# A hybrid attention, RWKV-7 and HGRN2 layer with experts on one core: order of the 64x64 matmuls between row halves

## The chip, the core and the metric

The kernel runs on one core of a Trainium2 chip. TensorE does the matmuls, reading its weights and moving data from SBUF and writing PSUM banks of 128 partitions by 512 f32; VectorE (DVE) and ScalarE (ACT) copy and process what lies in the banks, GpSimd (POOL) issues small transfers, and SyncE (SP) issues the large ones. The metric is the device time of one execution in microseconds; the median of the runs counts.

TensorE takes a matmul on a part of its array: the partitions that the operands lie in are its row part, the output partitions its column part. A "tile" here is such a part. With operands of 64 partitions and 64 output partitions there are four of them: row half 0 or 1 with column half 0 or 1. "Own" means that both halves have the same number, "other" that they differ.

## What is computed

Two groups of 128 tokens, a prompt and a sample, go through one layer with the same weights. Heads are split among attention, RWKV-7 and HGRN2; then come an output projection and 32 experts of which each token uses 4.

```python
# RWKV-7, both directions d
S = S * w_t + (S @ a_t) b_t^T + v_t k_t^T ;  y_t = S @ r_t
# HGRN2, chunkwise, both directions
att = einsum('ntd,nsd,ntsd->nts', q, k, dec) ;  o = att @ v + (q * exp(b)) @ S_before
# layer
x = x + gate1 * (concat(att, rwkv, hgrn) @ w_out)
x = x + gate2 * moe(norm(x))          # top 4 of 32, 1024 wide, clamped SwiGLU
```

The prompt starts from zero states, the sample from given ones. All is f32.

## The kernel before

The program is written by hand for each engine, in the order in which the engine runs it; semaphores join the engines. The eight PSUM banks are rotated: `open_bank` waits until the job that had the bank six jobs ago was read, `filled` signals a job as complete, `after` waits until it was read. Loops over s (0 the prompt, 1 the sample) and over two directions d are unrolled, and the four heads n lie in pairs, head n in row half n % 2 where its transposed data are used.

The sequence of TensorE is: modulation and input projections (to about 160 us), the mixers of the prompt, mixed with the input projections and the first levels, then the mixers of the sample (to about 338 us), the output projection (L938), the router, and from about 403 us a loop over the 32 experts (L1135, L1155), whose six weight blocks of 2 MB each stream through a ring of six slots. A slot is asked for again (L379) when its matmuls are done. The ring's memory serves as working memory of the mixers before, so that the second half of `w_out` is loaded into slot 0 only when `hg_done` is given, behind VectorE's copy L1708 of the last HGRN2 sum.

For each group the delta rule is solved with a 128-token triangle split into two halves of 64 rows: five levels of merges build an inverse (`rw_level_w` L667 and `rw_level_xy` L682, which alternate between the row halves), and then come the functions of this case, in this order for both groups:

- `rw_right`: right hand sides, matmuls with AKd (own, L717) and AKo (other, L721) and, for the sample, the initial state (L711). ScalarE then copies two blocks (L1267).
- `rw_first`: the first half solved (L734), in direction 0 row half 0, in direction 1 row half 1.
- `hg_scores(s, 2)`: HGRN2 scores of one pair of heads in one direction: one matmul for the pair of halves (`hg_off`, L832) and eight for four levels (L839), for each of two row halves q.
- `rw_carry` (L745), `rw_early_y` (L757 state, L763 own, L766 other), `rw_second` (L777), `hg_scores(s, 3)`, `rw_out` (L788 own, L790 other).
- for the prompt `rw_pairs` of the sample (L623, L634, L644) follows, and `hg_sum` (L856 state, L862 own, L865 other) later; for the sample `hg_sum` follows at once.

[...] There are 16 fences in all. The state matmuls have 128 output partitions (64x128); two for each direction and row half.

## Time and profile before

| | us |
|---|---|
| median of 3 runs (1364.95 to 1370.54) | 1368.74 |
| the profiled execution | 1370.94 |
| its span, first to last instruction | 1368.7 |
| TensorE matmuls busy | 1231.2 (90%) |
| VectorE busy | 311.4 (23%) |
| ScalarE busy | 228.7 (17%) |

[...] The DMA moves 427 to 429 GB/s from about 445 us to the end. [...]

### The profile page before, as it was taken

The page shows a single profiled execution, that of the slowest core. Times are in us where ns is not written, and L with a number is a line of the kernel's source. Part 1 is how long each engine was busy: PE and PEld are TensorE (multiplying, and loading weights), DVE is VectorE, ACT ScalarE, POOL GpSimd, SP SyncE. Part 2 cuts the span into 40 slices and gives each one's busy share as a digit, 9 for nine tenths or more (in the row PEclk, how much of TensorE's full clock was granted, in tenths as well). Part 3 has the DMA queues.
Part 4 walks back from the last instruction along what each step waited for, and adds up shares of the span by engine and source line. Part 5 has one row for each costly group of instructions (what it writes and reads, how often), then busy time and mean ns, then how long its engine had stood idle before and what let it go on. Part 6 is the DMA issues. An engine that isn't in the chain of part 4 may idle for free.

```text
span 1368.7 us, 17187 instructions
## 1 busy us (share of the span) xinstructions
PE 1231.2 (90%) x7074; PEld 513.1 (37%) x7074; DVE 311.4 (23%) x629; ACT 228.7 (17%) x381; POOL 37.9 (3%) x69
## 2 busy tenths in 40 slices
PE   3988999788869999999999999999999999999994
PEld 1333578668343333333233333233333333333331
DVE  1200655652230112111121111112111112111113
ACT  2110344343121111111111111111111111111112
POOL 0300000000000000000000000000000000000000
PEclk9998997885858999999999999999999999999998
DMA  9966300003945999999999999999999999999991
GB/s 372 321 253 219 140 1 3 10 4 124 386 169 245 428 427 428 426 429 429 428 426 427 428 429 426 428 427 428 429 427 427 428 427 428 428 427 427 428 429 76
DMA packets 44241, 459.93 MB, mean 336 GB/s; under 512 B 5113, under 2 KB 7329, under 8 KB 16433
## 3 DMA queue, kind: packets, MB, share of 16 engines
q1 hardware_dynamic: 41152, 451.98, 78.9%
q0 software_dynamic: 2576, 6.35, 1.7%
q10 hardware_dynamic: 480, 1.13, 0.2%
q8 instruction: 25, 0.41, 0.1%
q14 instruction: 8, 0.06, 0.0%
HBM read 457.96 MB, written 1.47 MB: 336 GB/s over the span
## 4 chain that ended last, share of the span: by engine, by line
DMA 50%; PE 42%; DVE 4%; ACT 2%; issue 1%; DVEq 0%; SPq 0%; ACTq 0%
DMA ring<-in_moe_w_gu_dram 45%; PE bank L1135 15%; DMA ring<-in_w_mod_dram 5%; PE bank L567 4%; PE bank L1155 4%; PE bank L938 2%; PE bank L544 2%; PE bank L682 1%; PE bank L1098 1%; PE bank L1113 1%; PE bank L557 1%; PE bank L839 1%; PE bank L1125 1%; PE bank L824 1%; PE bank L667 1%
## 5 line engine op out<-in xcount | busy, mean ns | idle before, releaser
L1135 PE MATMUL bank<-ring,proj 128*64 128x512 f32 x2048 | 459.0, 598 | 33.7 <-DMA ring<-in_moe_w_gu_dram 33.7
L1135 PEld LDWEIGHTS bank<-ring,proj 128*64 128x64 f32 x2048 | 140.3, 137 | 350.9 <-issue 274.7
L1155 PE MATMUL bank<-ring,proj 128*64 128x512 f32 x1024 | 233.8, 598 | 11.9 <-DVE proj L2011 11.9
L2002 DVE TENSOR_SCALAR proj<-bank 128x512 f32<-128x512 f32 x32 | 22.1, 692 | 484.6 <-PE bank L1135 484.6
L1491 ACT ACTIVATE proj<-proj 128x512 f32<-128x512 f32 x32 | 20.2, 630 | 605.3 <-DVE proj L2002 605.3
L1155 PEld LDWEIGHTS bank<-ring,proj 128*64 128x64 f32 x1024 | 69.0, 136 | 131.8 <-issue 131.8
L567 PE MATMUL bank<-ring,hT 128*128 128x512 f32 (+2 forms) x224 | 92.6, 571 | 4.3 <-DVE hT L1813 2.7
L2014 DVE COPY proj<-bank 128x512 f32<-128x512 f32 x32 | 22.1, 691 | 249.1 <-PE bank L1155 249.1
L1098 PE MATMUL bank<-h_nat,proj 128*64 128x512 f32 x264 | 64.0, 607 | 0.0
L1113 PE MATMUL bank<-proj 64*128 64x512 f32 x256 | 63.6, 615 | 0.0
L567 PEld LDWEIGHTS bank<-ring,hT 128*128 128x128 f32 x224 | 43.9, 200 | 52.3 <-issue 41.8
L544 PE MATMUL bank<-ring 128*32 128x512 f32 x192 | 30.9, 775 | 17.0 <-DMA ring<-in_w_mod_dram 16.7
L1106 PEld LDWEIGHTS bank<-const_sb,proj 128*128 128x128 f32 x260 | 34.3, 212 | 25.8 <-DVE proj L2009 24.3
L510 POOL DMA_DIRECT2D param_sb<-in_moe_b_gu_dram x32 | 17.7, 553 | 893.6 <-PE bank L1125 893.6
L1491 ACT ACT_TABLE_LOAD x32 | 41.1, 1283 | 0.6
L1106 PE MATMUL bank<-const_sb,proj 128*128 128x128 f32 x260 | 40.8, 300 | 0.0
L1113 PEld LDWEIGHTS bank<-proj 64*128 64x128 f32 x256 | 22.0, 186 | 41.0 <-issue 41.0
L938 PE MATMUL bank<-ring,hT 128*128 128x512 f32 x64 | 30.3, 635 | 6.9 <-DMA ring<-in_w_out_dram 6.1
L1125 PE MATMUL bank<-param_sb,const_sb 1*64 1x512 f32 x256 | 35.7, 627 | 0.8 <-ACT proj L1487 0.8
L1487 ACT ACTIVATE proj<-bank 128x512 f32<-128x512 f32 x33 | 19.7, 597 | 86.9 <-PE bank L1106 86.9
L2011 DVE COPY proj<-bank 128x512 f32<-128x512 f32 x32 | 22.1, 692 | 50.1 <-PE bank L1106 50.1
L1098 PEld LDWEIGHTS bank<-h_nat,proj 128*64 128x64 f32 x264 | 19.1, 139 | 38.2 <-issue 37.8
(333 smaller groups left out, 890.7 us busy)
## 6 DMA issues: line engine op xcount, KB each, us to landing
ring<-in_moe_w_gu_dram SPq DMA_DIRECT2D x128, 2048.0 KB, 24.4
ring<-in_moe_w_down_dram SPq DMA_DIRECT2D x64, 2048.0 KB, 21.7
ring<-in_w_mod_dram SPq DMA_DIRECT2D x12, 2048.0 KB, 10.1
ring<-in_w_in_dram SPq DMA_DIRECT2D x5, 2048.0 KB, 17.0
ring<-in_w_out_dram SPq DMA_DIRECT2D x2, 2048.0 KB, 7.7
const_sb<-in_constants_dram POOLq DMA_DIRECT2D x1, 2450.0 KB, 14.4
ring<-in_w_in_dram SPq DMA_DIRECT2D x1, 1536.0 KB, 6.6
ring<-in_w_in_dram SPq DMA_DIRECT2D x1, 1024.0 KB, 5.4
```

What stands on the lines that cost most here:

```text
L544: mm = pe.matmul(b[32 * q:32 * q + 32, :], keep["c_silu"].rearrange("p (c m) -> p c m", m=32)[:, k], ring[:, slot, kc * 2048 + q * 512:kc ...
L567: mm = pe.matmul(b[:, 0:w], hT[:, s, c, :], wv[:, c, :], start=(c == 0), stop=(c == KC - 1))
L938: mm = pe.matmul(b[:, :], hT[:, s, c, :], wv[:, c % 4, 512 * part:512 * part + 512], start=(c == 0), stop=(c == KC - 1))
L1098: mm = pe.matmul(b_misc[CAP * half:CAP * half + CAP, :], moe["hot"][:, CAP * s:CAP * s + CAP], h[:, s, 512 * half:512 * half + 512], start ...
L1106: mm = pe.transpose(out[:, P * c:P * c + P], cols[:, c, :], ident)
L1113: mm = pe.matmul(acc[2 * s + half][:, :], moe["scat"][rows, P * s:P * s + P], moe["y"][rows, :], start=False, stop=False, skip_group_check ...
L1125: mm = pe.matmul(b[CAP * half:CAP * half + CAP, :], ones[32 * q:32 * q + 1, 0:CAP], param[32 * q:32 * q + 1, 3 * D:3 * D + 512], start=Tru ...
L1135: mm = pe.matmul(b[CAP * half:CAP * half + CAP, :], xT[:, k % 4, k // 4, :], ring[:, j, 2048 * kc + o + 512 * half:2048 * kc + o + 512 * h ...
L1155: mm = pe.matmul(b_down[CAP * half:CAP * half + CAP, :], aT[:, k % 4, k // 4, :], ring[:, 4 + j, D * kc + 512 * half:D * kc + 512 * half + ...
L1491: A(moe["sig"], moe["glu"], ACT.Sigmoid, scale=ALPHA).then_inc(sem("sig_sb"), 1)
L2002: ts(moe["glu"], bank[4][:, :], LIMIT, None, ALU.min).then_inc(sem("glu_sb"), 1)
L2011: dve.tensor_copy(moe["actT"], bank[6][:, :]).then_inc(sem("actT_sb"), 1)
```

## The change

In `rw_right`, `rw_early_y`, `rw_out`, `hg_scores` and `hg_sum` the passes are no longer one for each row half. In one pass come the matmuls whose output half is their own row half, in the other those whose output half is the other one; inside a pass the row halves alternate. A fence stands between the passes. The state matmuls are split in two of 64 output partitions, the own one in the first pass and the other one in the second (`state_part`, and `begin` in `hg_sum`). `rw_out` does the pass with the other half first. In `rw_first`, `rw_carry` and `rw_second` the loops over heads and directions are exchanged, which makes their row halves alternate too.

```diff
+            def state_part(s, b, y, col, own, begun):
+
+                for n2 in range(2):
+                    for d in range(2):
+                        for r in range(2):
+                            o = r if own else 1 - r
+                            n = 2 * n2 + r
+                            mm = pe.matmul(b[part64(o), col(d, n)], T[part64(r), d, 0, n2, y, part64(o)], s0[part64(r), 2 * d + n2, :],
+                                           start=o not in begun, stop=False, skip_group_check=True)
+                            begun.add(o)
+                return mm
...
             def rw_right(s):
...
-                for r in range(2):
-                    if s:
-                        for d in range(2):
-                            for n in (r, 2 + r):
-                                cols = slice(256 * d + DH * n, 256 * d + DH * n + DH)
-                                pe.matmul(b[:, cols], T[part64(r), d, 0, n // 2, 0, :], s0[part64(r), 2 * d + n // 2, :],
-                                          start=not begun, stop=False, skip_group_check=True)
-                                begun |= {0, 1}
-                    for d in range(2):
-                        for n in range(4):
-                            cols = slice(256 * d + DH * n, 256 * d + DH * n + DH)
-                            mm = pe.matmul(b[part64(r), cols], AKd[part64(r), d, n, 0, :], vcols(s, n)[part64(r)],
+                    state_part(s, b, 0, col, True, begun)
+                for d in range(2):
+                    for n in range(4):
+                        for r in range(2):
+                            mm = pe.matmul(b[part64(r), col(d, n)], AKd[part64(r), d, n, 0, :], vcols(s, n)[part64(r)],
                                            start=r not in begun, stop=False, skip_group_check=True)
                             begun.add(r)
-                            if d == r:
-                                mm = pe.matmul(b[part64(1 - r), cols], AKo[part64(r), n, 0, :], vcols(s, n)[part64(r)],
-                                               start=1 - r not in begun, stop=False, skip_group_check=True)
-                                begun.add(1 - r)
-                    if r == 0:
-                        fence(mm)
+                fence(mm)
+                if s:
+                    state_part(s, b, 0, col, False, begun)
+                for n in range(4):
+                    for r in range(2):
+                        mm = pe.matmul(b[part64(1 - r), col(r, n)], AKo[part64(r), n, 0, :], vcols(s, n)[part64(r)],
+                                       start=False, stop=False, skip_group_check=True)
                 mm.then_inc(sem("rw_R1"), 1)
...
             def rw_first(s):
...
-                for d in range(2):
-                    for n in range(4):
+                for n in range(4):
+                    for d in range(2):
...
             def rw_out(s):
...
-                for r in (1, 0):
-                    for n in range(4):
-                        cols = slice(DH * n, DH * n + DH)
-                        for d in range(2):
-                            mm = pe.matmul(b[part64(r), cols], LRd[part64(r), d, n, 1, :], Ru[part64(r), d, n, :],
-                                           start=False, stop=False, skip_group_check=True)
-                        mm = pe.matmul(b[part64(1 - r), cols], LRo[part64(r), n, 1, :], Ru[part64(r), r, n, :],
-                                       start=False, stop=(r == 0), skip_group_check=True)
-                    if r == 1:
-                        fence(mm)
+                for n in range(4):
+                    for r in range(2):
+                        mm = pe.matmul(b[part64(1 - r), DH * n:DH * n + DH], LRo[part64(r), n, 1, :], Ru[part64(r), r, n, :],
+                                       start=False, stop=False, skip_group_check=True)
+                fence(mm)
+                for n in range(4):
+                    for d in range(2):
+                        for r in range(2):
+                            mm = pe.matmul(b[part64(r), DH * n:DH * n + DH], LRd[part64(r), d, n, 1, :], Ru[part64(r), d, n, :],
+                                           start=False, stop=(d == 1), skip_group_check=True)
                 filled(mm, "rw_y", s)
...
             def hg_scores(s, u):
...
-                for q in range(2):
-                    Uq = U[part64(q), u % 2]
-                    mm = pe.matmul(over[part64(d), DH * q:DH * q + DH], Uq[:, 1, 0, part64(d)], Uq[:, 0, 0, part64(1 - d)],
-                                   start=True, stop=True)
-                    if q:
-                        filled(mm, "hg_off", s, u)
+                def inside(own):
                     for l in range(1, 5):
-                        for blk in range(2):
-                            o = P * (l - 1) + DH * q
-                            mm = pe.matmul(b[part64(blk), o:o + DH], Uq[:, 1, l, part64(blk)], Uq[:, 0, l, part64(blk)],
-                                           start=True, stop=True)
-                    if q == 0:
-                        fence(mm)
-                filled(mm, "hg_att", s, u)
+                        for q in range(2):
+                            Uq, o, blk = U[part64(q), u % 2], P * (l - 1) + DH * q, part64(q if own else 1 - q)
+                            mm = pe.matmul(b[blk, o:o + DH], Uq[:, 1, l, blk], Uq[:, 0, l, blk], start=True, stop=True)
+                    return mm
+
+                off(0)
+                fence(inside(True))
+                filled(off(1), "hg_off", s, u)
+                filled(inside(False), "hg_att", s, u)
```

`rw_early_y` and `hg_sum` are changed as `rw_right` is. Nothing is changed on the other engines.

Below is TensorE's order in `rw_right` and the start of `rw_first` of the sample. Line numbers are those of the kernel that each belongs to; `x_res` holds the transposed factors T, `ring` AKd, AKo and the state, `proj` the values. Before (L711 state, L717 own, L721 other; a shape reads output partitions by columns):

```order
L711 MATMUL bank<-ring,x_res 128x64 x3
L717 MATMUL bank<-proj,ring 64x64
L721 MATMUL bank<-proj,ring 64x64
...
L717 MATMUL bank<-proj,ring 64x64 x4
L711 MATMUL bank<-ring,x_res 128x64 [waits pe_fence]
L711 MATMUL bank<-ring,x_res 128x64 x3
L717 MATMUL bank<-proj,ring 64x64 x5
L721 MATMUL bank<-proj,ring 64x64
...
L734 MATMUL bank<-hT,ring 64x64 [waits bank_free2,rw_Ysb,rw_Rsb]
```

After (L704 state, L726 own, L734 other, L744 `rw_first`):

```order
L704 MATMUL bank<-ring,x_res 64x64 x7
L726 MATMUL bank<-proj,ring 64x64 x16
L704 MATMUL bank<-ring,x_res 64x64 [waits pe_fence]
L704 MATMUL bank<-ring,x_res 64x64 x7
L734 MATMUL bank<-proj,ring 64x64 x8
L744 MATMUL bank<-hT,ring 64x64 [waits bank_free2,rw_Ysb,rw_Rsb]
```

Two state matmuls of 64 output partitions stand for one of 128, and the matmuls with AKo have moved behind the fence.

The second place is the end of `rw_out` and the `hg_sum` of the sample, on TensorE. Before (L788 and L790 `rw_out`, L856 state, L862 own, L865 other):

```order
L788 MATMUL bank<-hT,h_nat 64x64 x2
L790 MATMUL bank<-hT,h_nat 64x64
L856 MATMUL bank<-ring 128x64 [waits bank_free3,bank_free0,bank_free2,bank_free4,hg_attD]
L856 MATMUL bank<-ring 128x64 x3
L862 MATMUL bank<-proj,ring 64x64 x2
L865 MATMUL bank<-proj,ring 64x64
...
L856 MATMUL bank<-ring 128x64 [waits pe_fence]
L856 MATMUL bank<-ring 128x64 x3
```

After (L803 own pass of `rw_out`, L872 state, L882 own, L891 other):

```order
L803 MATMUL bank<-hT,h_nat 64x64 [waits pe_fence]
L803 MATMUL bank<-hT,h_nat 64x64 x15
L872 MATMUL bank<-ring 64x64 [waits bank_free3,bank_free0,bank_free2,bank_free4,hg_attD]
L872 MATMUL bank<-ring 64x64 x7
L882 MATMUL bank<-proj,ring 64x64 x16
L872 MATMUL bank<-ring 64x64 [waits pe_fence]
L872 MATMUL bank<-ring 64x64 x7
L891 MATMUL bank<-proj,ring 64x64 x8
```

The waits are the same, in front of the same functions; own and other matmuls stand apart, on either side of the fence.

## Rows read from the trace of the kernel before

**Rows 1.** Chain that ended last: shares by engine; pieces (start us, length us, what).

```profile
DMA 50%; PE 42%; DVE 4%; ACT 2%; issue 1%; DVEq 0%; SPq 0%; ACTq 0%
...
337.58 7.68 DMA ring<-in_w_out_dram
...
627.80 25.30 DMA ring<-in_moe_w_gu_dram
```

**Rows 2.** Waits of the load queue, 280 to 460 us: total, times, longest (us).

```profile
SPq L379 <- PE bank L1135: 62.5, 7, 44.0
```

**Rows 3.** Timeline: start us, us, engine, line, operation, count [idle before <- releaser].

```profile
220.66 0.27 PE L717 MATMUL bank<-proj,ring 64*64 64x64 f32 x1
...
223.89 1.17 PE L734 MATMUL bank<-hT,ring 64*64 64x64 f32 x13 [0.89 <-ACT hT L1267]
...
234.89 1.28 ACT L1203 ACT_TABLE_LOAD   x1
...
251.91 0.27 PE L862 MATMUL bank<-proj,ring 64*64 64x64 f32 x1
...
303.37 1.10 PE L711 MATMUL bank<-ring,x_res 64*128 64x64 f32 x8
...
314.62 1.96 PE L757 MATMUL bank<-ring,x_res 64*128 64x64 f32 x8
...
329.68 1.96 PE L856 MATMUL bank<-ring 64*128 64x64 f32 x8
...
337.52 0.42 DVE L1708 COPY mix<-bank 128x256 f32<-128x256 f32 x1 [5.40 <-PE bank L865]
```

**Rows 4.** Chain that ended last, within the mixers of both groups.

```profile
223.06 0.38 ACT hT L1267
...
239.22 0.44 DVE small L1645
...
246.15 1.10 PE bank L644 x32
...
254.27 1.88 PE bank L682 x62
```

**Rows 5.** Stretches: us, busy (records) of PE, others, granted clock, DMA.

```profile
223.10:223.90 0.80, 0.01 (x1) 0.01 (x1) 0.80 (x2) 0.71 (x2) 0.00 (x0) 1.00 0.00 0
223.90:225.00 1.10, 1.10 (x19) 1.10 (x22) 1.10 (x4) 0.00 (x0) 0.00 (x0) 0.57 0.00 0
...
303.40:305.60 2.20, 2.14 (x34) 1.94 (x33) 2.08 (x4) 0.00 (x0) 0.00 (x0) 1.00 0.00 0
305.60:309.00 3.40, 3.40 (x32) 3.23 (x32) 0.69 (x1) 0.00 (x0) 0.00 (x0) 0.56 0.38 89
...
285.00:289.00 4.00, 2.04 (x65) 1.00 0.01 2
```

**Rows 6.** Timeline of TensorE: runs that alternate, and L824, at either clock.

```profile
213.29 0.63 PE L839 MATMUL bank<-ring 64*64 64x64 f32 x15
...
276.36 3.68 PE L682 MATMUL bank<-ring 64*64 64x64 f32 x64 [3.73 <-DVE ring L1633]
279.96 2.59 PE L824 MATMUL bank<-const_sb,proj 128*128 128x512 f32 x4
...
283.56 1.56 PE L824 MATMUL bank<-const_sb,proj 128*128 128x512 f32 x4
...
287.08 2.08 PE L682 MATMUL bank<-ring 64*64 64x64 f32 x64 [1.96 <-DVE ring L1633]
```

**Rows 7.** Runs on one tile: chain piece at the high clock, timeline at the low.

```profile
221.34 0.47 PE bank L717 x8
...
228.94 0.53 PE L763 MATMUL bank<-proj,ring 64*64 64x64 f32 x3
...
229.36 0.86 PE L763 MATMUL bank<-proj,ring 64*64 64x64 f32 x3
```

**Rows 8.** Half a microsecond of TensorE with clock, DMA share and GB/s.

```profile
316.00:316.50 0.50, 0.50 (x3) 0.50 0.13 49
```

More of the change, by code:

```diff
@@ L851, in hg_sum, with begin @@
                 begun = set()
-                for r in range(2):
-                    if s:
-                        for n in (r, 2 + r):
-                            for d in range(2):
-                                pe.matmul(b[:, DH * n:DH * n + DH], inter[part64(r), 2 * d + n // 2, :], hst[part64(r), 2 * d + n // 2, :],
-                                          start=not begun, stop=False, skip_group_check=True)
-                                begun |= {0, 1}
-                    for n in range(4):
-                        cols = slice(DH * n, DH * n + DH)
-                        for d in range(2):
+                def begin(own):
+                    for n2 in range(2):
+                        for d in range(2):
+                            for r in range(2):
+                                o, n = r if own else 1 - r, 2 * n2 + r
+                                pe.matmul(b[part64(o), DH * n:DH * n + DH], inter[part64(r), 2 * d + n2, part64(o)],
+                                          hst[part64(r), 2 * d + n2, :], start=o not in begun, stop=False, skip_group_check=True)
+                                begun.add(o)
+                if s:
+                    begin(True)
+                for n in range(4):
+                    cols = slice(DH * n, DH * n + DH)
+                    for d in range(2):
+                        for r in range(2):
                             mm = pe.matmul(b[part64(r), cols], attD[part64(r), d, n, :], v[part64(r), cols],
@@ L864, in hg_sum @@
                             begun.add(r)
+                fence(mm)
+                if s:
+                    begin(False)
+                for n in range(4):
+                    cols = slice(DH * n, DH * n + DH)
+                    for r in range(2):
                         mm = pe.matmul(b[part64(1 - r), cols], attO[part64(r), n, :], v[part64(r), cols],
-                                       start=1 - r not in begun, stop=(r == 1), skip_group_check=True)
-                        begun.add(1 - r)
-                    if r == 0:
-                        fence(mm)
+                                       start=False, stop=True, skip_group_check=True)
                 filled(mm, "hg_o", s)
```

46 lines of the change are left out of this document (25 added, 21 removed).

## The prediction

> **What bounds the kernel now.** I read the chain that ended last first. From about 628 us on it is a relay of weight transfers, 25.30 us for the first, with short matmuls between, the expert loop at the DMA's rate; the line of shares has DMA at half of the chain [rows 1]. That stream can't start before the loop frees its first ring slot: the load queue's longest wait, 44.0 us, is for L1135 [rows 2]. So the kernel is a mixer of about 338 us, an output part and a stream of fixed length in a row, and what the mixer ends earlier the whole ends earlier. At the mixer's end TensorE's last sums (L865) release one VectorE copy, at 337.52, and the second half of the output weights is requested only then: 7.68 us in which nothing else can start [rows 1, 3]. That transfer's length stays and its start moves.
>
> Inside the mixer two stretches of the changed lines lie on the chain. A, the prompt group: from L717 at 220.66 to the VectorE reduce L1645 at 239.22, which waited for TensorE; behind it a chain of VectorE work leads to L644 at 246.15 [rows 3, 4]. B, the sample group: L711 at 303.37 to that copy at 337.52, TensorE busy nearly throughout [rows 3]. [...]
>
> **Prices.** An f32 matmul leaves two records. [...] Matmuls with the initial state (L711, L757, L856) are 64x128: 8 records take 1.10 us at the high level and 1.96 at the low, 0.14 and 0.245 each [rows 3].
>
> [...]
>
> **The change, part by part.** Fences stay 16 in number, one to a block, and cancel. No DMA, VectorE, ScalarE or GpSimd instruction changes. What changes is the order, and each state matmul splits in two: 24 of 64x128 become 48 of 64x64, 96 records. No row shows such a 64x64 state matmul; it lies between 0.0296/0.054 (any alternating 64x64) and 0.14/0.245 (its own old price). I take the low end, since L717, also a small one with a 64-row weight and 64 columns, runs at it where it alternates. Pass two alternates row half 0 to columns 1 with row half 1 to columns 0 in one bank, also unseen in this order: between 0.0296 and 0.059, and I take the low end, by L682, which writes one bank from both row halves.
>
> A, rw_right: 48 records, now from 220.66 until ScalarE's copy at 223.06 [rows 3, 4], 2.40 us; then 48 x 0.0296 + 0.25 + 0.2 = 1.87. Saves 0.5. Two ScalarE copies follow, and the idle time of 0.89 before L734 stays [rows 3]. From 223.89 to 239.22, 15.33 us, run 16 + 36 + 16 + 48 + 16 + 36 + 48 = 216 records and 4 fences. Short one-tile runs (L734, L745, L777) were already mixed with their neighbours by the engine, so I price the whole. At the low clock: 216 x 0.054 + 4 x 0.33 + 0.3 = 13.3, saves 2.1. At the high clock: 216 x 0.0296 + 4 x 0.25 + 0.2 = 7.6, saves 7.7, of which 0.3 is lost, since ScalarE's two table loads of 1.28, begun behind the last hg_scores, then end later than VectorE's reduce and its followers [rows 3].
>
> hg_sum of the prompt group, at the high clock: 251.91 to 254.27 for 48 records [rows 3, 4]; then 48 x 0.0296 + 0.25 = 1.7, saves 0.6.
>
> B, 34.15 us now. rw_right has 80 records, 80 x 0.0296 + 0.45 = 2.8; ScalarE's copies 0.9; then 248 records and 4 fences; then hg_sum, 80 and a fence. High clock: 2.8 + 0.9 + (7.3 + 1.0) + 2.8 = 14.8, saves 19.3. With the clock low from rw_right's end: 3.0 + 0.9 + (13.4 + 1.3) + 4.9 = 23.5, saves 10.7.
>
> Behind B is the transfer. Its cover is the first half of the weights and two spreads, landed by 316 us, when the DMA share falls to 0.13 [rows 8]; with all of A and B gone they would land some 2 us before the new request, so they do not bind yet.
>
> **The clock decides the size.** With the clock as now: 0.5 + 2.1 + 0.6 + 10.7 = 13.9. With it high through A and B: 0.5 + 7.4 + 0.6 + 19.3 = 27.8. What the rows say: in A the clock fell at about 224, after a rw_right of which 16 records of 48 ran alone on a tile and 0.8 us of idle time. In 285 to 289 TensorE also idled for 1.96 us and then ran alternating records (L682) without a break, and the clock stayed at 1.00 [rows 5, 6]. In B it fell after L711, eight records in a microsecond. The changed blocks alternate as L682 does there, and even with the ScalarE gap they are denser than either stretch in which it fell. So I take the high level through both. Against it: dense alternating records alone did not raise a clock that was down (L682 at 276.36, 3.68 us, all slow), so one fall costs the rest of its stretch. There is also a giving back: with A short, TensorE finishes its L634 work early and waits some 4 us for VectorE before L644; an idle time of 3.73 us before L682 at 276.36 put that run and the next at the low clock, (3.68 - 2.08) + (2.59 - 1.56) = 2.6 us [rows 6]. I book 2.6 as lost: 27.8 - 2.6 = 25.2.
>
> The profiled execution took 1370.94, its span 1368.7; the median shown is 1368.74, 2.2 lower. By the execution 1345.7; against the median, which I forecast: 1368.74 - 25.2 = 1343.5.
>
> **Rivals.** 1. The clock stays down in B only: 0.5 + 7.4 + 0.6 - 2.6 + 10.7 = 16.6, 1352; in A only: 22.5, 1346. Chance 0.22 together. 2. The clock goes as now: 1354.8, or 1356.7 if it falls before B's rw_right (80 x 0.054 + 0.6 = 4.9 instead of 3.0). Chance 0.16. 3. Pass two does not run in parallel: 336 records at double price, 128 of them where the clock is high now (3.8 us) and 208 where it is low (11.2), 15.0 against 13.9: 1369.8, no change. For it: no row has this order within one bank; against it L745, whose two tiles are these and whose records came closer than one-tile pace. Chance 0.05. [...] 4. Slower: a state record keeps its old price, being bound by its fetch and not by its width. Then 32 x 0.14 + 64 x 0.245 = 20.1 us stand for 10.6 now and 4.4 in my sum: 13.9 - 15.7 = -1.8, 1370.5; all 96 at 0.245, 13.9 - 19.1 = -5.2, 1373.9. It decides from 0.19 us a record on. Chance 0.04. 5. The gain is absorbed behind the mixer, because the stream or the ring waits for something fixed: 1362 to 1369. Against it the 44.0 us wait and the transfer at 337.58. Chance 0.03.
>
> **Numbers.** The forecast has 0.5. The range for 8 in 10 reaches from 1338.5 (no giving back, and cheaper fences) to 1357 (rival 2 with its early fall). A measurement of this kernel tells 0.5%, 6.8 us, from no change. Faster by more: 0.5 + 0.22 + 0.16 and a little of rival 5, 0.89. Within 0.5%: rivals 3 and 5, most of 4, 0.09. Slower by more: 0.02, for rivals 3 and 4 at once.
>
> **What would show it.** The clock in the new trace: 1.00 from L717's successor to the end of B's sums confirms the forecast; 0.5 behind the first ScalarE gap gives rival 2. Blocks of 80 records should take 2.8 us (high) or 4.9 (low), rw_out 1.9 or 3.2. Pass-two rows at 0.059 show rival 3, state rows at 0.14 rival 4. The VectorE reduce L1645 should start near 231, B last 15 us instead of 34, the weight transfer still 7.7, and the expert loop unchanged behind it. Wrong would be: a TensorE wait for hg_attD before hg_sum, since VectorE's four masked copies (1.3 us) have only 1.7 us of rw_out to hide in; or a different pattern of low clock between 246 and 303, which can give or take some 3 us.

## The result, and the profile after

| | before | changed |
|---|---|---|
| median, us | 1368.69 (4 runs) | 1345.62 (4 runs, 1345.12 to 1348.24) |
| ratio, 95% interval | | 0.9826 (0.9803 to 0.985) |
| the profiled execution, us | 1370.94 | 1348.24 |
| its span, us | 1368.7 | 1346.1 |

The change takes 23.1 us off the median. From here on six lengths are read from the trace of every kernel: the start of A (first matmul of the prompt's `rw_right`), A (to VectorE's reduce), the time between A and B, B (first matmul of the sample's `rw_right` to VectorE's copy of the last HGRN2 sum), the transfer behind it, and the rest.

| | start of A | A | between | B | transfer | rest |
|---|---|---|---|---|---|---|
| before | 220.7 | 18.56 | 64.15 | 34.15 | 7.68 | 1023.4 |
| changed | 222.2 | 10.22 | 64.91 | 18.23 | 7.76 | 1022.7 |
| difference | +1.6 | -8.34 | +0.76 | -15.92 | +0.08 | -0.7 |

The sum is -22.6 us, the difference of the spans. The program ahead of A and behind the transfer is the same in both. The lengths come from one profiled execution of each kernel; their spans differ by 22.6 us, the medians by 23.1.

The page of the changed kernel: span; busy time of TensorE; granted clock in 40 slices, in tenths; the line of chain shares.

```profile
span 1346.1 us, 17283 instructions
...
PE 1207.8 (90%) x7122; PEld 489.6 (36%) x7122; DVE 311.7 (23%) x629; ACT 228.8 (17%) x381; POOL 37.9 (3%) x69
...
PEclk8988899798859999999999999999999999999997
...
DMA 51%; PE 41%; DVE 4%; ACT 2%; issue 1%; DVEq 0%; SPq 0%; ACTq 0%
```

The 96 more instructions are the 48 additional records of TensorE, each with its weight load. The 24 additional matmuls leave 48 records, two each; so do the 16 of L726, x16 in the order and x32 in the timeline below. Its chain that ended last, start and length in us, which answers to [rows 1]; and the longest wait of the load queue, which answers to [rows 2]:

```profile
315.64 7.76 DMA ring<-in_w_out_dram
...
605.84 24.85 DMA ring<-in_moe_w_gu_dram
```

```profile
SPq L379 <- PE bank L1158: 69.2, 9, 44.0
```

The frame of the prediction stands. The transfer has its old length and starts 21.9 us sooner, the expert stream its old length and starts 22.0 us sooner, and the wait behind it is 44.0 us as before.

Stretch A in the timeline of the changed kernel (start us, us, engine, line, what, count, in brackets the idle time before and who ended it; L726 and L734 `rw_right`, L744 `rw_first`, L797 and L803 `rw_out`, L644 `rw_pairs`; VectorE's L1668 is the reduce that was L1645, its L1721 copies the HGRN2 scores). It answers to [rows 3, 4, 7]:

```profile
222.22 1.15 PE L726 MATMUL bank<-proj,ring 64*64 64x64 f32 x32
223.43 0.68 PE L734 MATMUL bank<-proj,ring 64*64 64x64 f32 x16
224.99 0.51 PE L744 MATMUL bank<-hT,ring 64*64 64x64 f32 x10 [0.88 <-ACT hT L1290]
...
230.23 0.63 PE L797 MATMUL bank<-hT,h_nat 64*64 64x64 f32 x16
230.93 1.08 PE L803 MATMUL bank<-hT,h_nat 64*64 64x64 f32 x29
...
230.97 1.31 DVE L1721 COPY_PREDICATED ring<-const_sb,bank 128x128 f32<-128x128 int32 x4 [0.51 <-DVE ring L1721]
232.44 0.42 DVE L1668 TENSOR_REDUCE small<-bank 128x4 f32<-128x256 f32 x1 [0.15 <-DVE ring L1721]
...
239.38 1.85 PE L644 MATMUL bank<-x_res 64*64 64x128 f32 x32 [3.67 <-DVE ring L1643]
```

Sixteen records in 0.63 to 0.68 us, 32 in 1.10 to 1.15: at a granted clock of 1.00 that is about 0.03 a record, in the own passes (L726, L803) and the other ones (L734, L797) alike. At a fence (the last matmul of a pass signals, and TensorE waits for the signal) it takes longer: L734 starts 1.21 us behind L726's first record, 0.26 more than 32 x 0.0296. The reduce is no longer released by TensorE but by VectorE's own queue of four masked copies, 0.15 us behind the last of them. And L644 starts after 3.67 us of idle time and takes 1.85 us instead of 1.10.

Stretch B (L704 state, L772 and L780 `rw_early_y`, L788 `rw_second`, L872 state of `hg_sum`, L891 its other pass, L1731 the copy that was L1708):

```profile
297.35 0.68 PE L704 MATMUL bank<-ring,x_res 64*64 64x64 f32 x16
297.86 1.10 PE L726 MATMUL bank<-proj,ring 64*64 64x64 f32 x32
299.03 0.68 PE L704 MATMUL bank<-ring,x_res 64*64 64x64 f32 x16
...
303.56 1.10 PE L772 MATMUL bank<-proj,ring 64*64 64x64 f32 x32
304.73 0.68 PE L704 MATMUL bank<-ring,x_res 64*64 64x64 f32 x16
305.24 0.28 PE L780 MATMUL bank<-proj,ring 64*64 64x64 f32 x4
307.72 0.51 PE L780 MATMUL bank<-proj,ring 64*64 64x64 f32 x7 [2.20 <-issue]
...
315.58 0.42 DVE L1731 COPY mix<-bank 128x256 f32<-128x256 f32 x1 [0.30 <-PE bank L891]
```

A state record costs 0.03 us like any other (16 in 0.68 us, as for L734). Inside a run of matmuls that wait for nobody stands a gap of 2.20 us, put down to "issue": nothing that the profile shows ended it. This is the new thing in this trace.

The clock, by stretches (length; busy time and records of PE, PEld, DVE, ACT, POOL; granted clock; DMA share; GB/s):

```profile
222.20:232.40 10.20, 8.98 (x297) 8.13 (x296) 8.83 (x21) 6.43 (x16) 1.16 (x2) 1.00 0.02 4
232.40:239.40 7.00, 2.15 (x77) 1.82 (x70) 6.20 (x16) 1.02 (x2) 0.00 (x0) 1.00 0.01 2
239.40:242.90 3.50, 3.50 (x40) 2.84 (x42) 3.27 (x5) 1.41 (x5) 0.00 (x0) 0.53 0.00 0
...
297.40:305.50 8.10, 7.01 (x217) 6.40 (x217) 3.96 (x9) 2.54 (x7) 0.00 (x0) 1.00 0.46 156
305.50:307.70 2.20, 0.02 (x2) 0.00 (x0) 0.00 (x0) 0.00 (x0) 0.00 (x0) 1.00 0.99 402
307.70:311.00 3.30, 3.21 (x67) 3.02 (x67) 0.00 (x0) 1.25 (x4) 0.00 (x0) 0.52 0.78 310
```

All of A is at a granted clock of 1.00, against 0.51 in 223.9 to 239.2 before. B is at 1.00 until the end of the gap and at 0.52 in the 3.3 us behind it; the first half of the output weights comes in meanwhile (DMA share 0.99 in the gap). High and low, up and down stand here for 1.00 and 0.50: half microseconds of before, 305.0 to 306.5, show 1.00, 0.97 and 0.50, and a value between comes from a stretch in which the clock changes.

### The profile page after: what moved, and what is told of

The parts are those of the page before. It is cut to its first block, busy times and chain, and to the rows that moved or that the text cites. A ratio compares the mean times of both kernels' runs of the same rounds, so it can differ in the third digit from the quotient of the medians.

```text
span 1346.1 us, 17283 instructions
## 1 busy us (share of the span) xinstructions
PE 1207.8 (90%) x7122; PEld 489.6 (36%) x7122; DVE 311.7 (23%) x629; ACT 228.8 (17%) x381; POOL 37.9 (3%) x69
## 4 chain that ended last, share of the span: by engine, by line
DMA 51%; PE 41%; DVE 4%; ACT 2%; issue 1%; DVEq 0%; SPq 0%; ACTq 0%
DMA ring<-in_moe_w_gu_dram 46%; PE bank L1158 15%; DMA ring<-in_w_mod_dram 5%; PE bank L567 4%; PE bank L1178 4%; PE bank L961 2%; PE bank L544 2%; PE bank L682 1%; PE bank L1121 1%; PE bank L1136 1%; PE bank L557 1%; PE bank L1148 1%; PE bank L667 1%; DMA ring<-in_w_out_dram 1%; PE bank L1196 1%
## 5 line engine op out<-in xcount | busy, mean ns | idle before, releaser
L1178 PE MATMUL bank<-ring,proj 128*64 128x512 f32 x1024 | 233.9, 598 | 11.9 <-DVE proj L2034 11.9
```

Of the source, the lines that this page charges most:

```text
L1178: mm = pe.matmul(b_down[CAP * half:CAP * half + CAP, :], aT[:, k % 4, k // 4, :], ring[:, 4 + j, D * kc + 512 * half:D * kc + 512 * half + ...
```

## The experiments

The kernels in one table; a median of one run is marked (1). p1 to p4 shared one chip and its runs of before (median 1369.48), p5 to p8 another set (1369.72), p9 to p11 a third (1368.81), p12 a fourth (1369.48).

| | median | ratio (95%) | start of A | A | between | B | transfer | rest |
|---|---|---|---|---|---|---|---|---|
| p1_right | 1352.93 | 0.9866 (0.9834 to 0.9898) | 225.5 | 11.84 | 66.68 | 26.27 | 7.68 | 1018.1 |
| p2_split | 1359.84 | 0.9919 (0.9892 to 0.9947) | 221.2 | 18.32 | 67.67 | 25.20 | 7.47 | 1022.2 |
| p3_scores | 1365.75 | 0.9981 (0.9962 to 1.0) | 216.5 | 13.58 | 65.68 | 31.32 | 7.57 | 1022.1 |
| p4_prompt_only | 1358.05 | 0.9893 (0.9856 to 0.9931) | 221.2 | 10.22 | 64.93 | 33.60 | 7.64 | 1020.3 |
| p5_sample_only | 1357.07 | 0.9893 (0.9856 to 0.993) | 221.7 | 18.65 | 66.18 | 18.26 | 7.72 | 1023.0 |
| p6_wout_mid | 1344.3 | 0.9819 (0.978 to 0.9859) | 219.8 | 10.22 | 64.90 | 14.40 | 11.98 | 1022.0 |
| p7_wout_late | 1350.64 (1) | | 221.0 | 10.23 | 64.92 | 14.39 | 15.04 | 1022.8 |
| p8_clock_down | 1361.81 (1) | | 231.5 | 12.95 | 67.06 | 18.03 | 7.75 | 1022.3 |
| p9_wout_fence | 1345.52 | 0.9827 (0.9809 to 0.9845) | 220.9 | 10.20 | 64.92 | 14.90 | 9.63 | 1023.3 |
| p10_wout_scores | 1343.24 | 0.9812 (0.9789 to 0.9834) | 219.2 | 10.21 | 64.91 | 17.72 | 7.69 | 1022.8 |
| p11_old_right | 1349.63 | 0.9865 (0.9847 to 0.9883) | 221.5 | 11.78 | 63.50 | 18.43 | 7.69 | 1021.9 |
| p12_spread_first | 1342.77 | 0.9796 (0.9775 to 0.9816) | 220.7 | 10.22 | 64.91 | 14.39 | 7.95 | 1022.3 |

Two things are to be seen before any verdict. All lengths of a row come from one profiled execution. With all blocks changed A takes 10.20 to 10.23 us in every trace where the clock is up, to a few hundredths. But the start of A scatters from 216.5 to 225.5 (p8 delays it on purpose) and the rest from 1018.1 to 1023.4, in parts of the program that no kernel touches. So a total says no more than its interval, and the verdicts below go by the stretches.

### One part of the change alone: rw_right

```diff
@@ before, function rw_right only: replaced by the new one, with state_part
-                for r in range(2):
-                    if s:
...
+                if s:
+                    state_part(s, b, 0, col, True, begun)
```

> The kernel before with only rw_right in its new order. Pace alone (clock as in the kernel before): the prompt's rw_right 1.9 us instead of 2.4, the sample's 2.8 to 3.0 instead of 5.8, in sum 3.4 us faster, about 1365.3. Theory of the clock (what TensorE did in and right behind rw_right decides whether it falls): the granted clock stays at 1.00 behind 224 us too, and the unchanged functions then run at the high level; the prompt's stretch from there to VectorE's reduce takes 9 to 10 us instead of 15.3 and the whole gains 8 to 20 us, 1349 to 1361.

16.6 us by the medians (14 to 23 by the interval). The paces of the prediction give rw_right 0.5 us in A and 2.9 in B. The stretches shortened by 6.7 and 7.9. The windows of this kernel say why (same columns as above; A, then B in two parts):

```profile
225.50:237.40 11.90, 10.67 (x287) 9.80 (x287) 8.85 (x22) 6.80 (x16) 1.16 (x2) 1.00 0.01 3
304.10:314.00 9.90, 8.82 (x195) 8.07 (x195) 3.96 (x9) 2.54 (x7) 0.00 (x0) 1.00 0.56 204
...
315.00:330.30 15.30, 15.08 (x169) 14.04 (x167) 3.24 (x10) 5.29 (x8) 0.00 (x0) 0.50 0.13 50
```

So of the two expectations the one on the clock came. A block of 48 records, made denser, keeps the clock up through 11.9 us in which every other block is the old one (granted clock 1.00; 0.51 in before's 223.9 to 239.2). In A the clock is then worth 6.72 - 0.5 = 6.2 of the 8.3 us that the whole change gains; the order of all other blocks adds only 11.84 - 10.22 = 1.6. In B the clock holds for 10 us and falls in the old `rw_early_y`. The 2.20 us gap does not appear, although the transfer runs (DMA share 0.56).

The other kernels bear it out: in the five with the old `rw_right` in A and no added wait (before, p2, p3, p5, p11) the clock falls 3.2 to 3.7 us behind the start of A, and in none of the eight with the new one (changed, p1, p4, p6, p7, p9, p10, p12) does it fall in A.

### The split of the state matmuls alone

```diff
-                                pe.matmul(b[:, cols], T[part64(r), d, 0, n // 2, 0, :], s0[part64(r), 2 * d + n // 2, :],
-                                          start=not begun, stop=False, skip_group_check=True)
-                                begun |= {0, 1}
+                                for o in (r, 1 - r):
+                                    pe.matmul(b[part64(o), cols], T[part64(r), d, 0, n // 2, 0, part64(o)], s0[part64(r), 2 * d + n // 2, :],
+                                              start=o not in begun, stop=False, skip_group_check=True)
+                                    begun.add(o)
```

and the same in `rw_early_y` and `hg_sum`; a pass stays one row half.

> The kernel before with only the state matmuls of the sample split in two of 64 output partitions; the passes stay one for each row half, so that a pair alternates between column halves of the same row half. Theory that any two tiles run side by side: 96 records at 0.03 to 0.054 us, 3 to 5.2 us in place of 10.6, so 5.4 to 7.6 us faster, 1361 to 1363.5. [...] Rival, the price hangs on the record and not on its width: 3 to 13 us slower.

9.6 us by the medians, B shorter by 8.95, A as before. Its state runs at either clock (they stood at 1.10 and 1.96 for x8 in [rows 3]):

```profile
307.17 0.68 PE L712 MATMUL bank<-ring,x_res 64*64 64x64 f32 x16
...
316.70 1.12 PE L759 MATMUL bank<-ring,x_res 64*64 64x64 f32 x16
```

Sixteen narrow records in 0.68 where eight wide ones took 1.10, 1.12 where they took 1.96. There are six such blocks. The first took 1.10 and the second, with the clock falling in it, 1.65 us before; both take 0.68 now. The others went from 1.96 to 1.12: 0.42 + 0.97 + 4 x 0.84 = 4.75 us. The rest of the 8.95 is put down to the clock, for the other records: it fell 6.5 us behind the start of B, against 2.6 before. Both matmuls of a pair lie in one row half and still overlap: 16 records in 0.68 us, against 8 in 0.47 on one tile [rows 7].

### hg_scores alone

```diff
-                for q in range(2):
-                    Uq = U[part64(q), u % 2]
...
+                off(0)
+                fence(inside(True))
+                filled(off(1), "hg_off", s, u)
+                filled(inside(False), "hg_att", s, u)
```

> The kernel before with only hg_scores in its new order (8 calls). Theory: its pairs alternated already (between column halves), 0 within 0.7 us. Rival (only different row groups overlap): 7 us faster.

Ten runs, 1359.06 to 1371.25: 3.7 us less by the medians, the interval from 0 to 5.2, so a small gain is possible and the rival's 7 is excluded. One run of 15 records in this kernel:

```profile
213.82 0.63 PE L840 MATMUL bank<-ring 64*64 64x64 f32 x15
```

It is the 0.63 us of the kernel before [rows 6]: alternating row halves and columns together is no faster than alternating columns in one row half. The profiled execution is the fastest of the ten; in it the clock of A was down for 3.4 microseconds only, and A took 13.58 us. That the clock can come back inside A, in a kernel whose records have the old pace, was the first sign against a step of the prediction.

### One group alone

```diff
+            def rw_right(s):
+                (rw_right_new if s == 0 else rw_right_old)(s)
...
```

and so for all eight functions; p4 has the new ones for the prompt, p5 for the sample.

> All changed functions in their new order for the prompt group, in their old order for the sample group. Theory: the prompt's stretch shortens by 8.3 us as in the trace of the changed kernel, of which up to 2 us go again to a low clock after TensorE's longer wait before L644; 6 to 8.5 us faster, about 1361.5; the sample's stretch stays at 34 us. If the clock of the prompt's stretch had nothing to do with it: 2.6 + 0.6 = 3.2 us faster.

> All changed functions in their new order for the sample group, old for the prompt group. Theory: the prompt's stretch stays at 18.6 us with its low clock, the sample's shortens from 34.2 to 15 to 18.5 us because its clock stays high; 15.5 to 19 us faster, 1350 to 1353. If the pace alone did it (clock low behind its first block): 10.7 us faster, 1358.

A in p4 is the 10.22 us of the full change, and its B 33.60 us, at the low level from 300 us on. In p5 B is 18.26 us, again with a gap of 2.2 us at the same matmul, and A 18.65. So each group's stretch shortens by its own order alone, 8.3 and 15.9 us, and nothing is carried over. By medians p4 gained 11.4 and p5 12.7; of p5's 15.9, 2.0 were lost between A and B, where the clock was down for longer (mean granted clock 0.81, against 0.88 in 239.3 to 303.4 of before). Rows of p4's B and of p5 in the gap:

```profile
300.00:329.80 29.80, 28.56 (x320) 26.61 (x318) 4.43 (x14) 7.83 (x15) 0.00 (x0) 0.50 0.29 107
```

```profile
316.91 0.52 PE L864 MATMUL bank<-proj,ring 64*64 64x64 f32 x7 [2.23 <-issue]
```

### What the gap of 2.2 us is

In three kernels (the changed one, p5 and p8) it sits behind the second matmul of `rw_early_y`'s other pass, 8.2 us into B, while the transfer runs. The next two kernels are the changed one with the request of the first half of `w_out` put off, so that the transfer does not run there.

```diff
             sp.wait_ge(sem("cache_out"), 32)
+            sp.wait_ge(full[jobs["rw_u", 1] % ROT], jobs["rw_u", 1] // ROT + 1)
             ring_load(4, w_out[:, 0:4, :])
```

(p6, until `rw_second` is complete; p7 in the same way until `rw_out` is complete, job `rw_y`.)

> The changed kernel, but the load queue waits for the sample's rw_second before it asks for the first half of the output weights (and the spreads behind it). The profiled changed kernel has a gap of 2.20 us in the middle of rw_early_y of the sample in which TensorE waits for no other engine, while this transfer runs and one instruction fetch is among its packets. Theory that the fetch waits behind the transfer: the gap is gone, the sample's stretch is 15 to 16 us instead of 18.3, and the transfer of the second half ends 0 to 2 us later; in sum 0 to 3 us faster than the changed kernel. Rival, the gap has another cause: the stretch stays at 18.3.

> The changed kernel with the first half of the output weights asked for only after the sample's rw_out, when nearly all of the sample's stretch is over. Fetch theory: no gap in the stretch, 15 us from L704 to VectorE's copy; rival: a gap of about 2 us as before. The wait for the weights behind it grows from 7.7 to about 13 us, so the whole is 2 to 4 us slower than the changed kernel.

The same place in p6 (L781 and L789 are the L780 and L788 of above), and all of its B:

```profile
302.76 0.46 PE L781 MATMUL bank<-proj,ring 64*64 64x64 f32 x10
303.01 0.27 PE L789 MATMUL bank<-hT,ring 64*64 64x64 f32 x2
```

```profile
294.90:309.20 14.30, 13.00 (x410) 11.97 (x409) 7.23 (x19) 5.04 (x12) 0.00 (x0) 1.00 0.30 105
```

No gap, no fall of the clock, B 14.40 us. So the gap comes with the transfer at that time, and it costs 3.83 us: 2.20 itself, 1.6 by the clock behind it. But the second half of the weights now queues behind the first: 11.98 us in p6, 15.04 in p7. B with the transfer takes 26.4 and 29.5 us against 26.05: one wait has been traded for another.

### A place for the transfer

p9 and p10 look for the time at which the first half can run without that.

```diff
             sp.wait_ge(sem("cache_out"), 32)
+            sp.wait_ge(sem("pe_fence"), 13)
             ring_load(4, w_out[:, 0:4, :])
```

is p9 (the fence of the sample's `rw_early_y`); p10 waits instead for the bank of the sample's third `hg_scores`, job `("hg_att", 1, 2)`.

> The changed kernel; only the request for the first half of w_out is put off until the fence of the sample's rw_early_y, 7.4 us behind the start of stretch B (3.2 in the changed kernel, 8.9 in p6_wout_mid). My theory: the 2.20 us in which TensorE waits for nothing the profile shows is its next instructions arriving late behind this transfer's packets. The request now comes when that place is nearly reached and its packets flow over 1 us later, so no such gap, B 14.4 us. The two halves and the spreads then need 17.5 us from the first request, as in p6_wout_mid: 24.9 us from B's start to the landing of the second half against 26.05 in the changed kernel. Time 1344.5. Rival (the gap belongs to this place in the code whatever the DMA does): gap of 2.2 stays, B 18.2, landing 26.0, 1345.6.

> The same request put off only until the sample's third hg_scores is complete, 5.5 us behind the start of B. If the packets are not yet dense when TensorE's next instructions are fetched, no gap: B 14.4 us, landing at 5.5 + 17.5 = 23.0 us from B's start, 3.0 less than the changed kernel, 1342.6. If they are dense enough, the gap is back in part or whole and with it the low clock behind it: B up to 18.2 us, landing 26.0, 1345.6. The rival of p9_wout_fence expects 1345.6 here as well.

p9 came as my theory had it: no gap at the old place, B and transfer 24.6 us, 1.5 less than in the changed kernel. p10 went half each way. The old place has no gap, but a second one appears, in `hg_sum`, at a matmul where p9 has a trace of it (first row p10, second p9, of the same instruction):

```profile
308.16 0.24 PE L873 MATMUL bank<-ring 64*64 64x64 f32 x1 [1.63 <-issue]
```

```profile
308.46 0.21 PE L873 MATMUL bank<-ring 64*64 64x64 f32 x1 [0.26 <-issue]
```

Two fixed places in the program, then. The traces say more of them if TensorE's own records are counted one by one in order of start (weight loads, matmuls, semaphores and the like). Before the gap stand 5313 of them in the changed kernel, in p5 and in p8, before the second place 5569 in p9 and p10: 256 more. And p8 has one instruction more ahead of B, its wait for the copies. There the gap lies one instruction earlier in the program, with four weight loads of `rw_early_y`'s other pass in front of it and not five (first row changed kernel, second p8):

```profile
305.18 0.25 PEld L780 LDWEIGHTS bank<-proj,ring 64*64 64x64 f32 x5
```

```profile
319.37 0.20 PEld L780 LDWEIGHTS bank<-proj,ring 64*64 64x64 f32 x4
```

So the place hangs on the count of instructions and not on a matmul or its data. That fits instructions that are themselves fetched by DMA, piece by piece: the page has a DMA queue of kind "instruction" with 25 packets, of 16,384 bytes each. One of them runs in 299.0 to 299.5 us of p6, 4.6 us into B, where no load is under way, and in 305.0 to 305.5 us of the changed kernel, 8.0 us into B, amid the load (first row p6, second changed; packets, MB, share of 16 engines):

```profile
q8 instruction: 1, 0.02, 15.8%
```

```profile
q8 instruction: 1, 0.02, 11.6%
```

The packet records of nine kernels, in us behind the start of B, with the time at which TensorE comes to the place and the time at which it goes on:

| | place | packet starts | landed | TensorE comes | goes on |
|---|---|---|---|---|---|
| changed | first | 7.96 | 8.88 | 8.18 | 10.37 |
| p5 | first | 7.95 | 8.88 | 8.18 | 10.40 |
| p8 | first | 7.87 | 8.80 | 8.18 | 10.28 |
| p10 | second | 11.37 | 12.33 | 12.19 | 13.82 |
| p9 | second | 10.03 | 10.91 | 12.19 | 12.45 |
| p6 | first | 4.57 | 5.83 | 8.2 | no gap |
| p7 | first | 4.83 | 6.21 | 8.2 | no gap |
| p1 | first | 7.89 | 8.82 | 11.3 | no gap |
| p11 | first | 9.63 | 10.61 | 12.3 | no gap |

In all five gaps, from 0.26 to 2.23 us long, TensorE goes on 1.5 us behind the landing, and where there is no gap it comes to the place later than that. The packet itself is late when the load is in flow: TensorE passes the instruction 256 ahead of the first place at 4.0 us in the changed kernel, p5 to p10, and the packet starts 0.6 to 1.1 us later in p6, p7, p9 and p10 and 3.9 to 4.0 us later in the changed kernel, p5 and p8. So the theory of the instruction fetch agrees with these traces in place, time and size. No record names the packet's content; that it holds TensorE's instructions is inferred. p1 and p11 have the load and no gap because their TensorE, slower on its way there, comes later.

The last kernel takes the load queue apart instead: the two spreads of the gate (1 MB) need neither place nor data from the mixer.

```diff
+            sp.wait_ge(free[jobs["rw_T", 1, 1, 1] % ROT], jobs["rw_T", 1, 1, 1] // ROT + 1)
+            for s in range(2):
+                spread(gate1[:, s, :], 2 * D, s, "gate1_in")
             sp.wait_ge(sem("at_done"), 1)
             sp.wait_ge(sem("cache_out"), 32)
+            sp.wait_ge(sem("pe_fence"), 13)
             ring_load(4, w_out[:, 0:4, :])
-            sp.wait_ge(free[jobs["rw_T", 1, 1, 1] % ROT], jobs["rw_T", 1, 1, 1] // ROT + 1)
-            for s in range(2):
-                spread(gate1[:, s, :], 2 * D, s, "gate1_in")
```

> The changed kernel with the load queue in another order: the two spreads of the gate (1 MB) are requested as soon as their place is free, before the attention of the sample ends, and the first half of w_out (2 MB) at the fence of the sample's rw_early_y as in p9_wout_fence. My theory (TensorE's next instructions come late only behind dense packets, and the second half of w_out waits for what is queued ahead of it): B as in p9_wout_fence or shorter, 14.4 to 14.9 us, with no gap of 2.2 us, and the second half takes 7.7 us after its request instead of 9.63, since only 2 MB are ahead of it: 22.3 us from B's start to its landing, against 24.5 in p9_wout_fence and 26.05 in the changed kernel. 1345.6 - 3.7 = 1341.9. Rival 1: the early spreads meet another fetch of instructions and bring a gap of about 2 us there: 1344. Rival 2 (the transfer's packets are not what matters): nothing is saved, 1345.6.

Its load queue, the chain at the transfer, and B:

```profile
214.61 0.82 SPq L383 DMA_DIRECT2D param_sb<-mod_rows  x2
```

```profile
310.31 7.95 DMA ring<-in_w_out_dram
```

```profile
295.90:310.20 14.30, 13.01 (x410) 11.98 (x410) 7.20 (x19) 5.06 (x12) 0.00 (x0) 1.00 0.40 148
```

The spreads go out at 214.6 us, ahead of A, and A is 10.22 us as ever. B is 14.39 us, without a gap and at a granted clock of 1.00 (the packet for the second place lands 10.25 us into B, TensorE comes there at 12.1), the transfer 7.95: together 22.4 us where 22.3 were expected and the changed kernel has 26.05. Its median of 1342.77 is the lowest of all. Against the changed kernel (ratios 0.9796 and 0.9826) the intervals overlap, so the total does not settle it; the stretches show the 3.65 us.

### The clock, let down on purpose

```diff
             hg_decay(0, 3)
+            pe.wait_ge(sem("late"), 7)
             rw_right(0)
...
+            for k in range(7):
+                A(hT_t[:, 1024:1536], hT_t[:, 1536:2048], ACT.Copy).then_inc(sem("late"), 1)
+                act.wait_ge(sem("late"), k + 1)
```

The first two lines are on TensorE, the others on ScalarE: seven copies ahead of the prompt's `rw_right`, for which TensorE stays idle for 5.58 us.

> The changed kernel with seven ScalarE copies (about 4.5 us) that TensorE waits for ahead of the prompt's rw_right, so that its clock falls before the stretch. Theory: an alternating order does not raise a clock that is down; the stretch behind that wait runs at the low level with 0.054 us a record: rw_right 3 us, from L744 to the reduce 13.3 us in place of 7.5, so that the kernel loses more than the wait, in sum 4 to 5 us of wait and 6 to 7 us of clock. Rival, the clock recovers within a few us: the stretch takes 8 to 10 us.

```profile
231.60:239.00 7.40, 6.32 (x108) 5.76 (x110) 1.25 (x4) 1.79 (x5) 0.00 (x0) 0.50 0.01 2
240.00:244.40 4.40, 4.19 (x146) 3.78 (x146) 1.36 (x5) 3.10 (x8) 1.17 (x2) 1.00 0.02 6
```

In the idle time the clock goes down: its mean is 0.82 in 225.9 to 231.5 and 0.50 from 231.6 to 239.0 (an idle time of 3.73 us has a slow run behind it in [rows 6]). But 8 us into A, inside the dense blocks, it is up again, and A takes 12.95 us: 2.7 more, and not the 5.7 of blocks at the low clock to the end.

### The change without rw_right

The changed kernel with `rw_right` as it was.

```diff
-                if s:
-                    state_part(s, b, 0, col, True, begun)
...
+                for r in range(2):
+                    if s:
+                        for d in range(2):
+                            for n in (r, 2 + r):
+                                cols = slice(256 * d + DH * n, 256 * d + DH * n + DH)
...
```

> The changed kernel with the rw_right of before (row half outermost, state matmuls 64x128). Theory (rw_right's one-tile runs are what let the clock fall in the kernel before, the rest is pace): the clock falls behind rw_right in both stretches although all other blocks alternate. A longer by 0.5 + 5.7 = 6.2 us, B by 2.4 + up to 8.5 = 10.9, given back up to 2.6: 1345.6 + 14.5 to 17 = about 1361. Rival (the whole sequence has to be dense or not, rw_right is one block of five): the clock stays up, only 0.5 + 2.4 are lost, 1348.5. Between: low in one of the stretches, 1352 to 1356.

In A and in B, two windows each:

```profile
225.00:228.00 3.00, 2.94 (x60) 2.75 (x58) 2.82 (x6) 1.03 (x3) 0.00 (x0) 0.50 0.02 5
229.00:233.20 4.20, 3.99 (x140) 3.58 (x138) 1.83 (x7) 3.01 (x7) 1.16 (x2) 1.00 0.03 6
...
300.00:306.00 6.00, 5.04 (x81) 4.60 (x82) 0.00 (x0) 1.79 (x5) 0.00 (x0) 0.50 0.83 300
307.00:315.10 8.10, 7.82 (x251) 7.20 (x247) 3.64 (x12) 3.19 (x7) 0.00 (x0) 1.00 0.31 121
```

Both theories are half right. The clock falls with the old `rw_right` again, right behind it in A and 3.1 us into B, still inside it, as mine had it. It comes back after 3.4 and 6.8 us of dense blocks, which mine excluded. The 1361 of mine was missed by 11 us, and the 1348.5 of the rival, for which the clock stays up, by 1.1. A is 1.56 us longer than with the new one, so the gains do not add up: the new `rw_right` alone takes 6.7 us off A (p1), the other blocks without it 6.8, both together 8.3. B is 4.0 us longer than a B without a gap; having met no gap it ends as late as the changed kernel's. The stretch between is 1.4 us shorter. The profiled execution is the fastest of the four runs (1347.06); the median is 4.0 us above the changed kernel's, and where the other three lost more the trace does not say.

## Why the prediction was right, and where it was off

The forecast was 1343.5, the result 1345.62, inside the range of 1338.5 to 1357.0. It was the forecast's case that came, except for 3.4 us in B: the clock high through A and most of B, pass two in parallel, state records at the small price. The clock, which the forecast called decisive, was: p1 shows it with one block.

- **The frame** (a mixer, one transfer, a stream in a row) held: transfer 7.68 and 7.76, the wait of 44.0 us the same, and the slices of both pages from about 445 us on at 426 to 429 GB/s, the last one apart (76 and 78).
- **The paces** held where they had no row: state records 0.03 us (rival 4 wanted 0.14), pass two 0.03 (rival 3 wanted 0.059). L734 writes one bank from both row halves, 16 records in 0.68 us at a granted clock of 1.00, and L797 does likewise (16 in 0.63); 8 records on one tile take 0.47. The other prices of the sum are in the rows of before: at the high clock 0.0296 us a record and a tail of 0.2 from 64 in 2.08 us (L682) and 15 in 0.63 (L839), (2.08 - 0.63)/49; at the low one 0.054 and a tail of 0.3 from 64 in 3.68 [rows 6]; on one tile 0.059 from 8 in 0.47 [rows 7].
- **The fences.** 0.33 us at the low clock is what two units of L763 and L766 show, 0.86 with a fence against 0.53 without [rows 7]. The 0.25 at the high clock was an estimate that no row shows; in the changed kernel the first record behind a fence starts 0.22 to 0.26 us later than the records ahead of it need at 0.0296 (L734 1.21 us behind the first of 32 records, L704 at 299.03 and at 304.73 1.17 behind the first of 32, L803 0.70 behind the first of 16).
- **hg_scores** has no term in the sum. p3 leaves at most 5.2 us, and the pace is unchanged (15 records in 0.63 us).
- **A**: 7.9 us were expected, 8.34 measured. The warning that TensorE might wait for the four masked copies ahead of `hg_sum` did not come true in B; in A the same copies hold up the reduce by a few tenths of a microsecond.
- **B** is the mis-sized term: 14.8 us were forecast and 18.23 came, 19.3 against 15.92 saved. The step that failed is the sentence that no DMA instruction changes, taken to mean that no DMA matters to TensorE. None changes, but the shorter B brings TensorE to a place in its program while the first half of `w_out` is coming in, and it stands still for 2.20 us, and behind that its clock is 0.52 for 3.3 us. The packet records point to an instruction fetch that starts 3.4 us later than in p6. Where the transfer is kept away B takes 14.39 (p7, p12), so the rest of the term was right to 0.4 us. I had costed the first half only as cover for the second; the same packets were never weighed against TensorE.
- **The giving back** was booked at 2.6 us, against 0.6 gained in the prompt's `hg_sum`; from L644 to the start of B the changed kernel takes 0.75 us more. The idle time ahead of L644 came (3.67, forecast some 4), the clock fell at it, and L644 took 1.85 instead of 1.10. What I left out is that before, the low clock of A ran on behind it, to 244.5, for 5.3 us, which the change removed.
- **Of the clock** one step was wrong without harm here: that dense alternating records do not raise a clock that is down, "so one fall costs the rest of its stretch". I had read it from one run of 3.68 us. p8, p11 and the changed kernel's own B (low for 3.4 us from 307.8 on) show it up again after 3.4 to 8.2 us of work. Rival 1 was therefore priced too high: one fall costs 1.6 to 2.7 us in A and not 5.7. What stays low for long does so among blocks with one-tile runs (15.3 us in A before, 29.8 us in the B of p4). Such runs do not decide it alone: in the A of p3, which has them too, the clock was back after 3.4 us.
- The start of A was 1.6 us later and the rest 0.7 shorter, in code that is the same; that is scatter and no part of the change.

The sum by terms: +0.4 in A, -3.4 in B, +1.2 between, -0.9 outside, against 25.2: 22.6. That the total is off by 2.1 us and not by the 3.4 of B is luck: A and the stretch between gave 1.6 more than forecast, scatter outside took 0.9, and the medians differ by 0.5 more than the profiled executions.

What stays open: what a fence guards against, since no kernel here leaves them out; what the 1.5 us between a packet's landing and TensorE's next instruction are, why the clock came back after 3.4 us in one kernel and not in 15 in another, and why p11's other three runs are slower than its profiled one.

## What to carry to other kernels

Small matmuls on quarters of the array cost half here when neighbours went to different quarters (0.03 us a record against 0.059, at a granted clock of 1.00), but the larger part of such a gain can be the clock: here one block of 48 records decided over 6 us behind it as long as the blocks there were the old ones (and 1.6 when they were new), so a block ought to be priced with the level that it leaves to its successors. When a stretch between transfers is shortened, look at what now runs beside what: a "released by issue" gap inside a run without waits, at the same instruction in several kernels, went away here by moving a transfer and not by touching TensorE. Count the instructions between two such places, and look when the packets of the instruction queue start and land. And move what is free to go early (here 1 MB of spreads) out from between two transfers of which the second is waited for.

## What the runs showed of the hardware that was not expected

- TensorE stood still 2.10 to 2.23 us at one fixed place, with a 2 MB load in full flow (402 to 410 GB/s in the gap), in the changed kernel, p5 and p8; 1.63 us in p10 and 0.26 in p9 at another one, 256 TensorE instructions on; and not at all at either in p6, p7 and p12. It went on 1.5 us behind the landing of a 16,384-byte packet of the instruction queue in all five. That packet started 0.6 to 1.1 us behind TensorE's passing of the instruction 256 ahead where no load ran, and 3.9 to 4.0 us behind it amid the load (both for the first place).
- Two matmuls with the same row half and different column halves overlap as well as two with different row halves: 15 records of L839 of before and 16 of L797 of the changed kernel both take 0.63 us. And 16 state records of 64 output partitions take 0.68 us (p2), against 1.10 for 8 of 128 (before).
- The granted clock came back from 0.50 to 1.00 in the middle of dense 64x64 work after 3.4 us (changed kernel, A of p11), 6.8 us (B of p11) and 8.2 us (p8), and did not in 15 and 30 us of work with one-tile runs in it (A before, B of p4); but in the A of p3, which has such runs, it did after 3.4 us.
- A stretch with the clock up repeats to a few hundredths of a microsecond in different kernels (10.20 to 10.23; 14.39 and 14.40), while the parts around it scatter by several.
